# A two-block transformer in float32 on one core: the statistics of its wide norms held with tokens on the partitions

## The chip, the cores and the metric

One core of a Trainium2 chip runs the whole program, one launch. The metric is device time in microseconds (us) of one execution, lower is better.

## What is computed

256 tokens of width 2048 go through two transformer blocks. The first mixes three branches (a gated convolution, chunked attention, attention over 256 memory tokens) and has a gated feed-forward part. The second has adaptive norms (shift and scale from a conditioning vector), four attention mixers of 512 columns each and a mixture of 16 experts. What matters here are the norms over all 2048 features:

```python
def rmsnorm(x, g):
    xf = x.astype(jnp.float32)
    y = xf * lax.rsqrt(jnp.mean(xf * xf, axis=-1, keepdims=True) + EPS)
    return (y * g.astype(jnp.float32)).astype(x.dtype)

    h = h + merged @ w_o[l]
    hn = rmsnorm(h, ffn_norm_g[l])                               # "ffn"
    ...
    h = h + (jax.nn.silu(gt) * val) @ w_down[l]
    return rmsnorm(h, final_norm_g)                              # "final"
    ...
    h = rmsnorm_2(x, norm1_g[l]) * (1.0 + sc1[:, None]) + sh1[:, None]   # "norm1"
    x = x + g1[:, None] * token_mixer(h, ...)
    h = rmsnorm_2(x, norm2_g[l]) * (1.0 + sc2[:, None]) + sh2[:, None]   # "norm2"
    x = x + g2[:, None] * moe_ffn(h, ...)
    return rmsnorm_2(x, final_g)                                 # "final2"
```

`norm1` follows `final` directly, so the kernel takes both roots at one place and applies `final` to the carried stream later.

## The kernel before

Activations lie with features on the 128 partitions and the 256 tokens along the free axis, 16 chunks of 128 features. Each f32 weight tile (128x2048) is split by ScalarE into a rounded part `w_hi` (`split`, L603) and by VectorE into the rest `w_lo` (`lo`, L1942); TensorE multiplies with both. Activations are split in the same way into `a_hi` and `a_lo`. There are four raw and four split buffers, and each engine's program is written out in order by hand: PE's block from L1192, VectorE's from L1929, ScalarE's from L595. Engines meet only through semaphores, and a wait holds up everything behind it on its engine.

A norm's sum of squares is taken over partitions: PE multiplies a 128x128 matrix of ones with the squares (`run_lane` L1370, `run_last` L1375). That gives the sum of every token in a full row of 256, the same on all 128 partitions (`psN`, in the bank `psO`). `root` (L1959 to L1963) forms mean plus EPS on 128x256 elements (VectorE), waits for ScalarE's square root (`std`, L712), and takes the reciprocal into `rstd` (L1962). `by_pairs` (L1981) then multiplies the 16 prescaled chunks two at a time by `rstd` and splits them, while ScalarE writes the upper parts (L701, L707). `root_both` (L1968 to L1974) does the same for `norm1` (a second row in `psM`) and leaves `final`'s root in `var`; its reciprocal is taken at step 11 of the second block's loop (L2536) and is applied from step 18 on. Behind the sums PE issues products of ones that nobody reads (`idle_products`, L1197): 14 at `ffn` and at `norm1`, 20 at `norm2`, none at `final2`, and 9 ahead of tile 3 of the second block.

The second block's loop runs over 58 weight tiles, step n for tile n, on PE (`second_half`, L1722), VectorE (L2521) and ScalarE (L1041). PE takes tiles 0 and 1 together. VectorE's step n first makes `w_lo` of tile n + 3. Before its step 0 it waits until ScalarE has copied out tile 0, and writes an input of the compression there (`cmp_in`, L2448). Its step 0 ends with L2458, its step 1 with a second `cmp_in`. ScalarE's `w_hi` of tile n + 4 waits for PE's end of tile n. At steps 5 and 7 PE turns the result of a gelu that VectorE makes from tile 3 and tile 5 (L1625).

Of the kernel before, what the change touches and what calls it, by code (L numbers as in the profile page):

```python
# [19 lines left out]
ALU = mybir.AluOpType  # L20
# [3 lines left out]
P = 128  # L24
S = 256
# [280 lines left out]

ROOTS = ["mem", "x", "lnvar", "ffn", "norm1", "final", "mixb", "mixd", "mixa", "mixc", "norm2", "final2"]
ROOT_AT = {n: k for k, n in enumerate(ROOTS)}
# [13 lines left out]
ADA_FIRST = 6  # L322
ADA_EACH = 9


# [5 lines left out]
def build(nc, tiles, ada_tiles, x_d, mem_d, params_d, crow_d, rel_rev, onehot_d, maskrow_d, ident_d,  # L331
          cmpmask_d, tab_d, sinks_d, rbias_d, router_d, gd_d, w2_d, pe_d, grp_d, tri_d, out, fbias_d):
    with ExitStack() as ctx:
# [6 lines left out]
        def sem(name):  # L340
# [34 lines left out]
        psF = psT[:, 0, 0:S]  # L375
        psM = psO[:, S:2 * S]

        landed = [sem(f"tile_landed{s}") for s in range(RAW)]
# [16 lines left out]
                 "gain_last_squares", "gain_sums", "rstd_ready", "normed_pairs", "tail_chunk",  # L395
                 "carried", "pre_ready", "rstd_columns", "rstd_columns_copied", "conv_lane", "centred_lane", "first_hi", "first_lo"]
        W = {n: sem(n) for n in names}
# [53 lines left out]
        def col(n):  # L451
            _cols[0] += n
            return small[:, _cols[0] - n:_cols[0]]
# [15 lines left out]
        cs = col(12)  # L469
        rcol = col(2)  # L470
        iota = col(NE)
        warm_root = col(1)
# [123 lines left out]
        def _(act):  # L596
# [301 lines left out]
            for k in range(DC):  # L898
# [8 lines left out]
            std("ffn")  # L907
            act.wait_ge(used, BASE["ffn"])
# [26 lines left out]
            def ffn_groups():  # L935
# [65 lines left out]

            act.wait_ge(W["variance_ready"], NORM_AT["norm1"] + 1)
            nc.scalar.activation(pool[:, VAR2, :], pool[:, VAR2, :], ACT.Sqrt, bias=zero, scale=1.0 / D)\
                .then_inc(W["std_ready"], 1)
            std("final")
            split(Tile(BASE["two"] + 2))
# [81 lines left out]
            for g in range(4):  # L1088
# [3 lines left out]
                for c in range(4 * g, 4 * g + 4):  # L1092
                    if g == 3:
                        if c < 15:
                            act.wait_ge(W["tail_chunk"], 3 + c - 11)
                        else:
# [3 lines left out]
                                         scale=scale2[:, c:c + 1]).then_inc(W["pre_ready"], 1)  # L1100
            std("norm2")
            act.wait_ge(used, BASE["moe"])
# [73 lines left out]
            for g in range(4):  # L1176
# [3 lines left out]
                for c in range(4 * g, 4 * g + 4):  # L1180
                    if g == 3:
                        if c < 15:
                            act.wait_ge(W["tail_chunk"], 6 + c - 11)
                        else:
# [3 lines left out]
                                         scale=pc("final2_g", c)).then_inc(W["pre_ready"], 1)  # L1188
            std("final2")


        @block.tensor  # L1192
        def _(pe):
            def idle_products(n, into=None):

                for _ in range(n):
                    nc.tensor.matmul(psS[:, 1, 0:P] if into is None else into, ones[:, :], ones[:, :],  # L1197
                                     start=True, stop=True)
# [158 lines left out]
            def norm_part(name, g, sq=SQ, into=psN):  # L1357
# [6 lines left out]
                last.then_inc(W["sums_part"], 1)  # L1364

            def run_lane(name, lane, into=psN, start=True):

                wait(pe, W["variance_ready"], NORM_AT[name])
                pe.wait_ge(W["lanes_added"], 3 * RUN.index(name) + 3)
                nc.tensor.matmul(into, ones[:, :], pool[:, lane, :], start=start, stop=False)  # L1370

            def run_last(name, c, sq, into=psN):

                pe.wait_ge(W["last_squares"], 4 * RUN.index(name) + c + 1)
                last = nc.tensor.matmul(into, ones[:, :], pool[:, sq + 4 + c, :], start=False,  # L1375
                                        stop=c == 3 and name != "final")
                if c == 3:
                    last.then_inc(W["sums_part"], 3)
# [160 lines left out]
            run_last("ffn", 3, SQ)  # L1539
            idle_products(14)  # L1540

            def ffn_groups():
# [42 lines left out]
                for c in range(4):  # L1585
                    nc.tensor.matmul(psM, ones[:, :], pool[:, GAIN_SQ + c, :], start=c == 0, stop=False)
                pe.wait_ge(W["gain_lanes"], 2)
                nc.tensor.matmul(psM, ones[:, :], pool[:, GAIN_LANE, :], start=False, stop=False)
                wait(pe, W["variance_ready"], NORM_AT["final"])
                for c in range(4):  # L1590
                    if c == 3:
                        pe.wait_ge(W["lanes_added"], 3 * RUN.index("final") + 3)
                        nc.tensor.matmul(psN, ones[:, :], pool[:, FINAL_LANE, :], start=False, stop=False)
                    run_last("final", c, US)
                    pe.wait_ge(W["gain_last_squares"], c + 1)
                    last = nc.tensor.matmul(psM, ones[:, :], pool[:, GAIN_SQ + 4 + c, :], start=False, stop=c == 3)
                last.then_inc(W["gain_sums"], 1)
                idle_products(14)

# [324 lines left out]
            for n in range(4):  # L1924
                big_down(NE - 1, n)
            run_sums("final2", HF, 56, psF)


        @block.vector  # L1929
        def _(dve):  # L1930
# [24 lines left out]
            def root(name, width, src=psN):  # L1955
# [7 lines left out]
                dve.wait_ge(W["rstd_ready"], ROOT_AT[name] + 1)  # L1963

            def root_both():

                dve.wait_ge(W["gain_sums"], 1)
                nc.vector.tensor_scalar(var[:, :], psN, 1.0 / D, EPS, ALU.mult, ALU.add)\  # L1968
                    .then_inc(W["variance_ready"], 1)
                dve.wait_ge(W["variance_ready"], NORM_AT["final"] + 1)  # L1970
                nc.vector.scalar_tensor_tensor(pool[:, VAR2, :], var[:, :], EPS * D, psM, ALU.mult, ALU.add)\
                    .then_inc(W["variance_ready"], 1)
                dve.wait_ge(W["std_ready"], NORM_AT["final"])
                nc.vector.reciprocal(pool[:, RSTD2, :], pool[:, VAR2, :]).then_inc(W["rstd_ready"], 1)  # L1974
                dve.wait_ge(W["rstd_ready"], ROOT_AT["norm1"] + 1)

# [297 lines left out]
            dve.wait_ge(emptied["D"], OWN[:BASE["ffn"]].count("D"))  # L2274
            root("ffn", D)
            dve.wait_ge(W["pre_ready"], 16)
            by_pairs("ffn", PRE, rstd[:, :])

# [150 lines left out]
            root_both()  # L2429
            by_pairs("norm1", PRE, pool[:, RSTD2, :], bias=mod[:, 0:16])  # L2430
            lo(Tile(BASE["two"] + 2))
# [89 lines left out]
            for n, (kind, what, x) in enumerate(SECOND):  # L2521
# [58 lines left out]
                .then_inc(W["router_lo"], 1)  # L2580
            root("norm2", D)
            dve.wait_ge(W["pre_ready"], 32)
            by_pairs("norm2", PRE, rstd[:, :], bias=mod[:, 48:64])
            dve.wait_ge(W["router_turned"], 1)
# [136 lines left out]
            for n in range(4):  # L2721
                expert_add(NE - 1, n)
            root("final2", D, psF)
            dve.wait_ge(W["pre_ready"], 48)
            for p in range(8):
                y = chunks(PRE + 2 * p, 2)
                nc.vector.tensor_tensor(y, y, rstd[:, :].unsqueeze(1).to_broadcast([P, 2, S]), ALU.mult)\
                    .then_inc(W["final_ready"], 1)
# [259 lines left out]
```

## Time and profile before

| | us |
|---|---|
| median of 3 runs | 2922.99 |
| lowest and highest | 2920.28, 2929.36 |
| the profiled execution, its own time | 2924.94 |
| its span, first to last instruction | 2923.1 |
| PE (TensorE) busy | 2864.7 (98%) |
| DVE (VectorE) busy | 2171.5 (74%) |
| ACT (ScalarE) busy | 1510.5 (52%) |
| one split of a weight tile, mean: ScalarE, VectorE | 1.91, 2.30 |

The profile is of one execution. A page gives busy times, a picture of the span in 40 slices, the chain of work that ended last, and the costliest groups of instructions; the trace behind it can be asked for the instructions of a stretch in order of time. An f32 product appears as two records (two passes). Ends of PE's records are modelled and overlap, so starts are the safer numbers. The granted clock is 1.00 at TensorE's full 2.4 GHz and 0.50 at 1.2 GHz.

### The profile page before, as it was taken

Reading aid. Unit: us, or ns where it says so; the run is one execution under the profiler, and the core shown is the slowest. Engines: PE = TensorE matmul, PEld = TensorE weight load, DVE = VectorE, ACT = ScalarE, POOL = GpSimd, SP = SyncE. Lnnn points to the kernel's source line nnn. Section 1 sums busy time; section 2 is a strip of 40 time slices with the busy share of each in tenths; the row PEclk is TensorE's granted clock in tenths of the full one; section 3 lists DMA queues with packets and bytes.
Section 4 is the critical chain, followed back from the end, with each engine's and each line's share of the span. In section 5 each row is a group of like instructions: output and inputs, shape, how many; then the busy total and the mean of one; then the engine's idle time right before and its main releaser. Section 6 shows DMA issues by size and latency. Waiting matters only on the chain.

```text
span 2923.1 us, 45813 instructions
## 1 busy us (share of the span) xinstructions
PE 2864.7 (98%) x18030; PEld 2582.3 (88%) x18030; DVE 2171.5 (74%) x2675; ACT 1510.5 (52%) x1716; POOL 157.6 (5%) x228
## 2 busy tenths in 40 slices
PE   8999999999999999999999999999999999999998
PEld 8888888888888899999999989998989889889887
DVE  5644459998875899999999984665865876875874
ACT  5444564445554544444444464556554664664763
POOL 3000010000101000000000020111010000000001
PEclk9999999999999999999999999999999999999999
DMA  7445445555463978888788756444325885885982
GB/s 282 174 157 183 169 160 179 184 185 187 172 233 130 366 310 323 323 329 329 315 328 329 293 174 248 172 156 156 133 86 218 332 329 216 336 314 215 356 313 78
DMA packets 115681, 692.27 MB, mean 237 GB/s; under 512 B 14240, under 2 KB 27792, under 8 KB 34768
## 3 DMA queue, kind: packets, MB, share of 16 engines
q1 hardware_dynamic: 109952, 675.33, 61.1%
q10 hardware_dynamic: 4688, 11.01, 1.2%
q0 software_dynamic: 896, 3.93, 0.4%
q8 instruction: 99, 1.62, 0.2%
q14 instruction: 46, 0.38, 0.0%
HBM read 679.74 MB, written 10.49 MB: 236 GB/s over the span
## 4 chain that ended last, share of the span: by engine, by line
PE 88%; DVE 6%; ACT 3%; issue 2%; DMA 1%; SPq 0%; DVEq 0%; ACTq 0%
PE psT L1223 22%; PE psT L1224 11%; PE psT L1210 6%; PE psT L1212 6%; PE psT L1211 6%; PE psT L1332 3%; PE psT L1826 3%; PE psT L1828 3%; PE psT L1827 3%; PE psT L1816 2%; PE psT L1815 2%; PE psT L1817 2%; DVE w_lo L1942 2%; PE psY L1867 1%; PE psY L1866 1%
## 5 line engine op out<-in xcount | busy, mean ns | idle before, releaser
L1942 DVE TENSOR_TENSOR w_lo<-raw,w_hi 128x2048 fp32r<-128x2048 f32 x532 | 1220.0, 2297 | 369.4 <-ACT w_hi L603 364.8
L603 ACT ACTIVATE w_hi<-raw 128x2048 fp32r<-128x2048 f32 x532 | 1015.5, 1910 | 394.9 <-PE psT L1212 133.5
L1223 PE MATMUL psT<-a_both,w_hi 128*128 128x512 f32 x3072 | 1092.6, 400 | 9.6 <-DVE a_both L1992 2.8
L1224 PE MATMUL psT<-a_both,w_lo 128*128 128x256 f32 x3072 | 863.4, 281 | 0.0
L1223 PEld LDWEIGHTS psT<-a_both,w_hi 128*128 128x128 f32 x3072 | 578.7, 188 | 152.8 <-issue 8.7
L1224 PEld LDWEIGHTS psT<-a_both,w_lo 128*128 128x128 f32 x3072 | 581.7, 189 | 0.3
L1210 PE MATMUL psT<-a_both,w_hi 128*128 128x256 f32 x784 | 228.8, 292 | 9.2 <-DVE pool L2103 4.4
L1212 PE MATMUL psT<-a_both,w_lo 128*128 128x256 f32 x784 | 223.8, 285 | 0.0
L1211 PE MATMUL psT<-a_both,w_hi 128*128 128x256 f32 x784 | 223.6, 285 | 0.0
L2289 DVE CUSTOM_DVE_ANT_0 pool<-pool 128x2048 f32<-128x2048 f32 x96 | 219.0, 2281 | 4.9 <-DVE mod L2299 4.9
L1210 PE MATMUL psT<-h_hi,w_hi 128*128 128x256 f32 x752 | 214.7, 286 | 1.8 <-DVE pool L2305 1.1
L1211 PE MATMUL psT<-h_lo,w_hi 128*128 128x256 f32 x752 | 213.2, 284 | 0.0
L1212 PE MATMUL psT<-h_hi,w_lo 128*128 128x256 f32 x752 | 213.1, 283 | 0.0
L1210 PEld LDWEIGHTS psT<-a_both,w_hi 128*128 128x128 f32 x784 | 152.3, 194 | 10.7 <-DVE w_lo L1942 4.6
L1211 PEld LDWEIGHTS psT<-a_both,w_hi 128*128 128x128 f32 x784 | 152.3, 194 | 0.3
L1212 PEld LDWEIGHTS psT<-a_both,w_lo 128*128 128x128 f32 x784 | 152.1, 194 | 0.0
L1826 PE MATMUL psT<-w_hi,xw_hi 128*128 128x512 f32 x384 | 150.7, 393 | 0.0
L1828 PE MATMUL psT<-w_hi,xw_lo 128*128 128x512 f32 x384 | 149.6, 389 | 0.0
L1827 PE MATMUL psT<-w_lo,xw_hi 128*128 128x512 f32 x384 | 149.5, 389 | 0.0
L1210 PEld LDWEIGHTS psT<-h_hi,w_hi 128*128 128x128 f32 x752 | 144.8, 193 | 4.0 <-DVE pool L2305 1.4
L1815 PE MATMUL psT<-a_both,w_hi 128*128 128x256 f32 x512 | 146.0, 285 | 0.0
L1816 PE MATMUL psT<-a_both,w_hi 128*128 128x256 f32 x512 | 145.4, 284 | 0.0
(390 smaller groups left out, 4606.9 us busy)
## 6 DMA issues: line engine op xcount, KB each, us to landing
raw<-tiles_dram SPq DMA_DIRECT2D x532, 1024.0 KB, 5.0
pool<-ada_tiles_dram SPq DMA_DIRECT2D x96, 1024.0 KB, 4.9
bias_rows_dram<-pool ACTq DMA_DIRECT2D x1, 8192.0 KB, 56.5
pool<-bias_rows_dram SPq DMA_DIRECT2D x40, 128.0 KB, 4.5
pool<-bias_rows_dram SPq DMA_DIRECT2D x40, 64.0 KB, 4.6
pool<-mem_dram SPq DMA_DIRECT2D x4, 512.0 KB, 8.0
raw<-tiles_dram SPq DMA_DIRECT2D x8, 256.0 KB, 8.0
pool<-x_dram ACTq DMA_DIRECT2D x1, 2048.0 KB, 11.1
```

Source lines behind the costliest of these rows:

```text
L603: nc.scalar.activation(w_hi[:, t.k % SPL, :], raw[:, t.k % RAW, :], ACT.Copy).then_inc(hi_done, 1)
L1210: nc.tensor.matmul(ps_out, wh, x_hi, start=first, stop=False)
L1211: nc.tensor.matmul(ps_out, wh, x_lo, start=False, stop=False)
L1212: return nc.tensor.matmul(ps_out, wl, x_hi, start=False, stop=last)
L1223: nc.tensor.matmul(dst.rearrange("p (h s) -> p h s", h=2), wh, a_both[:, :, a, :], start=first, stop=False)
L1224: return nc.tensor.matmul(dst[:, 0:S], wl, a_hi[:, a, :], start=False, stop=last)
L1815: nc.tensor.matmul(dst, wh, a_hi[:, k, :], start=k == 0 and n % 2 == 0, stop=False)
L1826: nc.tensor.matmul(dst, xw_hi[:, k, :], wh, start=k == 0, stop=False)
L1827: nc.tensor.matmul(dst, xw_hi[:, k, :], wl, start=False, stop=False)
L1828: last = nc.tensor.matmul(dst, xw_lo[:, k, :], wh, start=False, stop=k == DC - 1)
L1942: nc.vector.tensor_tensor(w_lo[:, t.k % SPL, :], raw[:, t.k % RAW, :], w_hi[:, t.k % SPL, :].bitcast(F32), ALU.subtract).then_inc(lo_done, 1)
L2289: nc.vector.tensor_tensor_reduce(out=buf, in0=buf, in1=flat(CROW, 8), scale=1.0, scalar=0.0, op0=ALU.mult, op1=ALU.add, accum_out=ada_acc[ ...
```

## The change

For `ffn`, `norm1`, `final`, `norm2` and `final2` the squares become the stationary operand and one column of ones the moving one: two products 128x1 per chunk, one for each 128 tokens. The sums then stand in two columns, tokens on the partitions. Mean, root and reciprocal work on 128x2 elements in `small`. PE spreads the two columns back: `stat_rows` uses the column, broadcast to 128x128, as weights and the identity as moving operand, into `psRows` (part of `psP`, a PSUM bank), and VectorE's multiplications read their factor there. The four narrow mixer norms and those ahead of `ffn` stay as they were.

```diff
+            def token_std(name, at=0, scale=1.0):
+                act.wait_ge(W["variance_ready"], NORM_AT[name] + 1)
+                nc.scalar.activation(stat[:, at:at + 2], stat[:, at:at + 2], ACT.Sqrt, bias=zero, scale=scale)\
+                    .then_inc(W["std_ready"], 1)
...
+            def token_sums(into, src, start=False, stop=False):
+                for tt in range(2):
+                    last = nc.tensor.matmul(into[:, tt:tt + 1], src[:, tt * P:tt * P + P], ones[:, 0:1],
+                                            start=start and tt == 0, stop=stop and tt == 1)
+                return last
+
+            def stat_rows(name):
+                pe.wait_ge(W["stat_ready"], STATS.index(name) + 1)
+                for tt in range(2):
+                    last = nc.tensor.matmul(psRows[:, tt * P:tt * P + P],
+                                            stat_r[:, tt:tt + 1].to_broadcast([P, P]), ident[:, :], start=True, stop=True)
+                last.then_inc(W["stat_rows"], 1)
...
             run_last("ffn", 3, SQ)
-            idle_products(14)
+            idle_products(8)
+            stat_rows("ffn")
+            idle_products(6)
...
                 last.then_inc(W["gain_sums"], 1)
-                idle_products(14)
+                idle_products(8)
+                stat_rows("norm1")
+                idle_products(8)
...
                     gelu_turned(n // 7)
+                if n == 2:
+                    stat_rows("final")
                 second_half(n, 0)
...
             run_sums("norm2")
-            idle_products(20)
+            idle_products(8)
+            stat_rows("norm2")
+            idle_products(12)
...
             run_sums("final2", HF, 56, psF)
+            stat_rows("final2")
...
+            def rows_of(name, at):
+                nc.vector.reciprocal(stat_r[:, 0:2], stat[:, at:at + 2]).then_inc(W["stat_ready"], 1)
+                dve.wait_ge(W["stat_rows"], STATS.index(name) + 1)
+
+            def token_root(name, src=psN):
+                m = NORM_AT[name]
+                dve.wait_ge(W["sums_part"], SQ_AT[name] + GROUPS[name])
+                nc.vector.tensor_scalar(stat[:, 0:2], src[:, 0:2], 1.0 / D, EPS, ALU.mult, ALU.add)\
+                    .then_inc(W["variance_ready"], 1)
+                dve.wait_ge(W["std_ready"], m + (1 if m < NORM_AT["lnmean"] else 0))
+                rows_of(name, 0)
...
-            by_pairs("ffn", PRE, rstd[:, :])
+            by_pairs("ffn", PRE, psRows)
...
                 attend(SECOND_UNITS, 20, SC2, Q2, ticks_at(n, 0, N_UNITS + 4))
-                if n == 11:
+                if n == 1:
                     dve.wait_ge(W["std_ready"], NORM_AT["norm1"])
-                    nc.vector.reciprocal(rstd[:, :], var[:, :]).then_inc(W["rstd_ready"], 1)
+                    rows_of("final", 0)
+                    nc.vector.tensor_copy(rstd[:, :], psRows).then_inc(W["rstd_ready"], 1)
                     dve.wait_ge(W["rstd_ready"], ROOT_AT["final"] + 1)
```

Where instructions move, their order tells more than the diff. VectorE, steps 0 and 1 of the second block's loop, before: `w_lo` of tile 3, `h_lo`, `w_lo` of tile 4, the second `cmp_in`.

```order
L1942 TENSOR_TENSOR w_lo<-raw,w_hi 128x2048 [waits tile_hi_done]
L2458 TENSOR_TENSOR h_lo<-pool,h_hi 128x480 [waits cmp_hi]
L1942 TENSOR_TENSOR w_lo<-raw,w_hi 128x2048 [waits tile_hi_done]
L2448 TENSOR_TENSOR pool<-pool 64x8x15 [waits cmp_lo,sums_emptied_act]
L2448 TENSOR_TENSOR pool<-pool 64x8x15 x7
L1942 TENSOR_TENSOR w_lo<-raw,w_hi 128x2048 [waits tile_hi_done] x2
```

The same place in the changed kernel (each line number is the new file's):

```order
L1981 TENSOR_TENSOR w_lo<-raw,w_hi 128x2048 [waits tile_hi_done]
L2510 TENSOR_TENSOR h_lo<-pool,h_hi 128x480 [waits cmp_hi]
L1981 TENSOR_TENSOR w_lo<-raw,w_hi 128x2048 [waits tile_hi_done]
L2006 RECIPROCAL small<-small 128x2 [waits std_ready]
L2589 COPY rstd<-psY 128x256 [waits stat_rows]
L2500 TENSOR_TENSOR pool<-pool 64x8x15 [waits cmp_lo,sums_emptied_act,rstd_ready]
L2500 TENSOR_TENSOR pool<-pool 64x8x15 x7
L1981 TENSOR_TENSOR w_lo<-raw,w_hi 128x2048 [waits tile_hi_done] x2
```

Behind `w_lo` of tile 4 there is now the small reciprocal, and a copy that waits for PE.

PE at the same place in the changed kernel, from the end of tile 1 to the start of tile 2:

```order
L1220 MATMUL psT<-a_both,w_hi 128x256
L1221 MATMUL psT<-a_both,w_lo 128x256
L1386 MATMUL psY<-ident,small 128x128 [waits stat_ready,tile_lo_done]
L1386 MATMUL psY<-ident,small 128x128
L1219 MATMUL psT<-a_both,w_hi 128x256 [waits sums_emptied_act,tile_lo_done]
L1220 MATMUL psT<-a_both,w_hi 128x256
```

The two spreading products stand ahead of tile 2; before, L1212 of tile 1 was followed directly by L1210 of tile 2.

PE behind the sums of `norm2`, before:

```order
L1370 MATMUL psY<-pool,ones 128x256 [waits lanes_added,variance_ready]
L1375 MATMUL psY<-pool,ones 128x256 [waits last_squares] x4
L1197 MATMUL psY<-ones 128x128 x20
L1610 MATMUL psY<-a_both,h_hi 16x256 [waits ident_r_set,act_lo_ready,variance_ready,router_lo]
```

and in the changed kernel, from the last chunk's squares on:

```order
L1378 MATMUL psY<-ones,pool 128x1 [waits last_squares]
L1378 MATMUL psY<-ones,pool 128x1
L1206 MATMUL psY<-ones 128x128 x8
L1386 MATMUL psY<-ident,small 128x128 [waits stat_ready]
L1386 MATMUL psY<-ident,small 128x128
L1206 MATMUL psY<-ones 128x128 x12
L1644 MATMUL psY<-a_both,h_hi 16x256 [waits ident_r_set,act_lo_ready,variance_ready,router_lo]
```

The spreading products stand behind eight idle ones, and twelve follow them ahead of the router's first product.

## Rows read from the trace of the kernel before

**Rows 1.** Page, part 4: shares by engine of the chain that ended last.

```profile
PE 88%; DVE 6%; ACT 3%; issue 2%; DMA 1%; SPq 0%; DVEq 0%; ACTq 0%
```

**Rows 2.** Timeline at `norm2` (start us, us, engine, line, op, tiles, shapes, count, [idle before]).

```profile
2150.78 0.67 PE L1375 MATMUL psY<-pool,ones 128*128 128x256 f32 x2 [0.19 <-ACT pool L679]
...
2151.29 4.63 PE L1197 MATMUL psY<-ones 128*128 128x128 f32 x40
2151.49 0.43 DVE L1959 TENSOR_SCALAR var<-psY 128x256 f32<-128x256 f32 x1 [2.19 <-PE psY L1375]
2151.95 0.42 ACT L712 ACTIVATE var<-var 128x256 f32<-128x256 f32 x1 [0.82 <-DVE var L1959]
...
2152.40 1.75 DVE L1962 RECIPROCAL rstd<-var 128x256 f32<-128x256 f32 x1 [0.48 <-ACT var L712]
2154.19 1.29 DVE L1981 TENSOR_TENSOR pool<-pool,rstd 128x512 f32<-128x512 f32 x2
```

**Rows 3.** Groups by form on VectorE: busy us, mean ns of one | idle before.

```profile
L2231 DVE TENSOR_TENSOR pool<-psT,pool 128x512 f32<-128x512 f32 x24 | 16.5, 689 | 13.2 <-ACT pool L861 13.2
...
L2038 DVE TENSOR_SCALAR small<-small 128x2 f32<-128x2 f32 x68 | 11.5, 169 | 2.4
...
L2054 DVE RECIPROCAL small<-small 128x2 f32<-128x2 f32 x68 | 10.8, 159 | 0.5
L1981 DVE TENSOR_TENSOR pool<-pool,rstd 128x512 f32<-128x512 f32 x16 | 10.8, 683 | 0.1
```

**Rows 4.** Group by form on ScalarE.

```profile
L747 ACT ACTIVATE small<-small 128x1 f32<-128x1 f32 x16 | 4.5, 280 | 0.0
```

**Rows 5.** Timeline, PE: 128x1 products on f32 weights, two tiles of tokens.

```profile
62.42 0.50 PE L1477 MATMUL psY<-ident,rstd 128*128 128x1 f32 x4
```

**Rows 6.** Timeline at `ffn`.

```profile
939.97 3.29 PE L1197 MATMUL psY<-ones 128*128 128x128 f32 x28
940.99 0.42 DVE L1959 TENSOR_SCALAR var<-psY 128x256 f32<-128x256 f32 x1
...
943.67 1.29 DVE L1981 TENSOR_TENSOR pool<-pool,rstd 128x512 f32<-128x512 f32 x2
```

**Rows 7.** Timeline at `final2`, the end of the program.

```profile
2912.07 0.42 DVE L1959 TENSOR_SCALAR var<-psT 128x256 f32<-128x256 f32 x1 [2.52 <-PE psT L1375]
...
2914.76 4.90 DVE L2727 TENSOR_TENSOR pool<-pool,rstd 128x512 f32<-128x512 f32 x8
```

**Rows 8.** Timeline at `norm1`.

```profile
1713.98 3.29 PE L1197 MATMUL psY<-ones 128*128 128x128 f32 x28
1714.43 0.41 DVE L1968 TENSOR_SCALAR var<-psY 128x256 f32<-128x256 f32 x1
...
1717.66 1.29 DVE L1981 TENSOR_TENSOR pool<-pool 128x512 f32<-128x512 f32 x2
...
1719.62 0.35 PE L1210 MATMUL psT<-a_both,w_hi 128*128 128x256 f32 x1 [2.35 <-DVE a_both L2005]
```

**Rows 9.** Timeline on VectorE, start of the second block's loop.

```profile
1733.01 2.60 DVE L2448 TENSOR_TENSOR pool<-pool 64x120 f32<-64x120 f32 x8 [1.32 <-ACT pool L1077]
...
1738.42 2.28 DVE L1942 TENSOR_TENSOR w_lo<-raw,w_hi 128x2048 fp32r<-128x2048 f32 x1
```

**Rows 10.** Timeline on PE, same place.

```profile
1733.05 0.36 PE L1210 MATMUL psT<-a_both,w_hi 128*128 128x256 f32 x1 [0.21 <-ACT pool L1077]
...
1738.87 2.17 PE L1197 MATMUL psY<-ones 128*128 128x128 f32 x18
```

**Rows 11.** Timeline on PE, start of tile 5 of the second block.

```profile
1752.04 0.24 PE L1625 MATMUL psY<-ident,pool 30*128 30x30 f32 x1 [2.32 <-DVE pool L2474]
```

**Rows 12.** Windows: us, busy (x instructions) of PE, PEld, DVE, ACT, POOL, granted clock, DMA, GB/s.

```profile
2178.00:2180.00 2.00, 1.87 (x10) 1.88 (x10) 0.07 (x1) 0.00 (x0) 0.00 (x0) 0.50 0.96 406
...
2186.00:2188.00 2.00, 2.00 (x12) 2.00 (x11) 1.79 (x2) 2.00 (x2) 0.00 (x0) 0.52 1.01 426
...
1720.00:1724.00 4.00, 4.00 (x23) 4.00 (x23) 4.00 (x10) 2.68 (x7) 0.00 (x0) 0.57 0.00 0
```

More of the change, by code:

```diff
@@ L305 @@
     _at += GROUPS[_name]
-ROOTS = ["mem", "x", "lnvar", "ffn", "norm1", "final", "mixb", "mixd", "mixa", "mixc", "norm2", "final2"]
+ROOTS = ["mem", "x", "lnvar", "final", "mixb", "mixd", "mixa", "mixc"]
 ROOT_AT = {n: k for k, n in enumerate(ROOTS)}
@@ L323 @@
 ADA_EACH = 9
+STATS = ["ffn", "norm1", "final", "norm2", "final2"]
 def ada_place(k):
@@ L376, in build @@
         psM = psO[:, S:2 * S]
+        psRows = psP[:, 0:S]
         landed = [sem(f"tile_landed{s}") for s in range(RAW)]
@@ L470, in build @@
         rcol = col(2)
+        stat, stat_r = col(4), col(4)
         iota = col(NE)
@@ L906, in _ @@
                                      scale=pc("ffn_norm_g", k)).then_inc(W["pre_ready"], 1)
-            std("ffn")
+            token_std("ffn")
             act.wait_ge(used, BASE["ffn"])
@@ L1000, in _ @@
             ffn_groups()
[L1002 to L1005, printed above, removed]
+            token_std("norm1", 2, 1.0 / D)
+            token_std("final")
             split(Tile(BASE["two"] + 2))
@@ L1100, in _ @@
                                          scale=scale2[:, c:c + 1]).then_inc(W["pre_ready"], 1)
-            std("norm2")
+            token_std("norm2")
             act.wait_ge(used, BASE["moe"])
@@ L1188, in _ @@
                                          scale=pc("final2_g", c)).then_inc(W["pre_ready"], 1)
-            std("final2")
+            token_std("final2")
         @block.tensor
@@ L1369, in run_lane @@
                 pe.wait_ge(W["lanes_added"], 3 * RUN.index(name) + 3)
+                if name in STATS:
+                    token_sums(into, pool[:, lane, :], start)
+                    return
                 nc.tensor.matmul(into, ones[:, :], pool[:, lane, :], start=start, stop=False)
@@ L1374, in run_last @@
                 pe.wait_ge(W["last_squares"], 4 * RUN.index(name) + c + 1)
-                last = nc.tensor.matmul(into, ones[:, :], pool[:, sq + 4 + c, :], start=False,
-                                        stop=c == 3 and name != "final")
+                stop = c == 3 and name != "final"
+                if name in STATS:
+                    last = token_sums(into, pool[:, sq + 4 + c, :], False, stop)
+                else:
+                    last = nc.tensor.matmul(into, ones[:, :], pool[:, sq + 4 + c, :], start=False, stop=stop)
                 if c == 3:
@@ L1592, in ffn_groups @@
                         pe.wait_ge(W["lanes_added"], 3 * RUN.index("final") + 3)
-                        nc.tensor.matmul(psN, ones[:, :], pool[:, FINAL_LANE, :], start=False, stop=False)
+                        token_sums(psN, pool[:, FINAL_LANE, :])
                     run_last("final", c, US)
                     pe.wait_ge(W["gain_last_squares"], c + 1)
-                    last = nc.tensor.matmul(psM, ones[:, :], pool[:, GAIN_SQ + 4 + c, :], start=False, stop=c == 3)
+                    last = token_sums(psM, pool[:, GAIN_SQ + 4 + c, :], False, c == 3)
                 last.then_inc(W["gain_sums"], 1)
-                idle_products(14)
+                idle_products(8)
+                stat_rows("norm1")
+                idle_products(8)
             ffn_groups()
@@ L1963, in root @@
                 dve.wait_ge(W["rstd_ready"], ROOT_AT[name] + 1)
+            def rows_of(name, at):
[8 more added lines that the diff above has]
+                rows_of(name, 0)
             def root_both():
                 dve.wait_ge(W["gain_sums"], 1)
-                nc.vector.tensor_scalar(var[:, :], psN, 1.0 / D, EPS, ALU.mult, ALU.add)\
+                nc.vector.tensor_scalar(stat[:, 0:2], psN[:, 0:2], 1.0 / D, EPS, ALU.mult, ALU.add)\
                     .then_inc(W["variance_ready"], 1)
                 dve.wait_ge(W["variance_ready"], NORM_AT["final"] + 1)
-                nc.vector.scalar_tensor_tensor(pool[:, VAR2, :], var[:, :], EPS * D, psM, ALU.mult, ALU.add)\
+                nc.vector.scalar_tensor_tensor(stat[:, 2:4], stat[:, 0:2], EPS * D, psM[:, 0:2], ALU.mult, ALU.add)\
                     .then_inc(W["variance_ready"], 1)
                 dve.wait_ge(W["std_ready"], NORM_AT["final"])
-                nc.vector.reciprocal(pool[:, RSTD2, :], pool[:, VAR2, :]).then_inc(W["rstd_ready"], 1)
-                dve.wait_ge(W["rstd_ready"], ROOT_AT["norm1"] + 1)
+                rows_of("norm1", 2)
             def by_pairs(name, src, rows, bias=None):
@@ L2274, in _ @@
             dve.wait_ge(emptied["D"], OWN[:BASE["ffn"]].count("D"))
-            root("ffn", D)
+            token_root("ffn")
             dve.wait_ge(W["pre_ready"], 16)
-            by_pairs("ffn", PRE, rstd[:, :])
+            by_pairs("ffn", PRE, psRows)
             nc.vector.memset(us[:, :, 0:2], 0.0).then_inc(W["pairs_read"], 2)
@@ L2429, in _ @@
             root_both()
-            by_pairs("norm1", PRE, pool[:, RSTD2, :], bias=mod[:, 0:16])
+            by_pairs("norm1", PRE, psRows, bias=mod[:, 0:16])
             lo(Tile(BASE["two"] + 2))
@@ L2580, in _ @@
                 .then_inc(W["router_lo"], 1)
-            root("norm2", D)
+            token_root("norm2")
             dve.wait_ge(W["pre_ready"], 32)
-            by_pairs("norm2", PRE, rstd[:, :], bias=mod[:, 48:64])
+            by_pairs("norm2", PRE, psRows, bias=mod[:, 48:64])
             dve.wait_ge(W["router_turned"], 1)
@@ L2722, in _ @@
                 expert_add(NE - 1, n)
-            root("final2", D, psF)
+            token_root("final2", psF)
             dve.wait_ge(W["pre_ready"], 48)
@@ L2726, in _ @@
                 y = chunks(PRE + 2 * p, 2)
-                nc.vector.tensor_tensor(y, y, rstd[:, :].unsqueeze(1).to_broadcast([P, 2, S]), ALU.mult)\
+                nc.vector.tensor_tensor(y, y, psRows.unsqueeze(1).to_broadcast([P, 2, S]), ALU.mult)\
                     .then_inc(W["final_ready"], 1)
```

6 lines of the change are left out of this document (3 added, 3 removed).

## Prediction

> **What bounds the kernel now.** I read the chain of work that ended last first: 88% of it is PE [rows 1]. A change pays only where PE stands still or where its last work is released late, and it costs wherever it makes PE wait. The norms are such places: PE has nothing to multiply until the first chunks are normalised. So I read the four norms in order of time, then the stretch of the second block into which the change puts a new wait.
>
> At `norm2` [rows 2] the reader is to see a relay. The last squares go through PE at 2150.78, VectorE adds EPS at 2151.49 (0.43 us), ScalarE takes the root at 2151.95 (0.42), VectorE the reciprocal at 2152.40 (1.75), and the first multiplication starts at 2154.19. That is 2.70 us from sum to use, 1.75 of it one reciprocal of 256 elements. Beside it run 40 records of idle products, 4.63 us, 0.116 each. At `ffn` the same relay takes 943.67 - 940.99 = 2.68 us [rows 6], at `norm1`, with one step more, 1717.66 - 1714.43 = 3.23 [rows 8], at `final2` 2914.76 - 2912.07 = 2.69 [rows 7].
>
> **The small steps.** On 128x2 elements VectorE needs 0.17 us for a tensor_scalar and 0.16 for a reciprocal [rows 3]. For the root I take 0.28, from the nearest row, 128x1 on ScalarE [rows 4]. With hand-overs of 0.03 to 0.04 us, as between the rows of `norm2`, this makes 0.17 + 0.04 + 0.28 + 0.03 + 0.16 = 0.68 us. Then the spreading is new: two f32 products, four records. Four records of 128x1 took 0.50 us [rows 5]; with 128 moving columns at 0.116 each and the drain of the last I take 0.6, between 0.5 and, at half the clock, 1.0. The sums themselves: two products of 128x1 per chunk are four records, 0.50 us, instead of two records of 256 columns, 0.67 us [rows 2, 5]. The last sum comes 0.15 us sooner, and PE's time is the same within 0.02 us per chunk, which I leave out.
>
> The multiplications now read their factor in PSUM. A tensor_tensor of this shape with one operand in PSUM takes 689 ns, without one 683 ns [rows 3]; I cost this at nothing (8 x 6 ns at `final2`). The Trainium skill speaks against it: "VectorE: DVE Perf Modes", section on the TRN2 errata, gives a fixed 120 cycles at 0.96 GHz for a PSUM source and 58 for SBUF, by which (an estimate) each multiplication would cost 65 ns more, `final2` 0.5 us, and the total would come out 0.5 us or a little more above mine. Here the rows decide: 6 ns.
>
> **Norm by norm.** The spreading products stand behind eight idle products, 16 records, and PE works in order. So each start is the later of two times.
>
> - `ffn`: the small steps are through at 940.99 + 0.68 = 941.67. The idle products start at 939.97, 0.118 each, and eight are through at 941.85. Plus 0.6 and a hand-over: 942.5 instead of 943.67, a gain of 1.2. What follows is a relay of VectorE and ScalarE that sets when PE gets its next tiles, so I let it through whole.
> - `norm1`: 1714.43 + 0.68 + 0.21 for the second small step = 1715.32. Idle products: 1713.98 + 1.88 = 1715.86. Start 1716.5 instead of 1717.66, a gain of 1.15.
> - `norm2`: the small steps end at 2152.0, but eight idle products only at 2151.29 + 1.86 = 2153.15. Start 2153.8 instead of 2154.19, a gain of 0.4. The twelve idle products behind may hold the router's first product some tenths longer, but its last one waits for VectorE. Bounds 0 and 0.6.
> - `final2`: no idle products. 2912.07 - 0.15 + 0.68 = 2912.6, 0.1 until PE has it, 0.6 to spread: 2913.3 to 2913.4 instead of 2914.76. I take 1.3; at half the clock 0.95. Nothing runs beside it, so it reaches the end whole.
>
> **`final`, the new wait.** Here the change does more than it says. The reciprocal that leaves step 11 (again 1.75 us of VectorE, as in [rows 2]; it lay beside a busy PE) gains nothing. But PE must now have the result of VectorE's step 1 before it may begin tile 2. Before, PE began tile 2 at 1733.05 [rows 10], and VectorE ended `w_lo` of tile 4 only at 1738.42 + 2.28 = 1740.70 [rows 9].
>
> Step by step. After `norm1` PE had stood idle for 2.35 us [rows 8], and then 4 us ran at a mean granted clock of 0.57 [rows 12], a mix of 2.4 and 1.2 GHz that lost 0.43 x 4 = 1.7 us. Now PE restarts at 1719.62 - 1.15 = 1718.5, and idle products last until about 1718.3; I take it that the clock holds. Tiles 0 and 1 end 1.15 + 1.7 = 2.85 us sooner, near 1729.7. VectorE's first `cmp_in` waits for ScalarE's copy of tile 0; VectorE itself is free 1.32 us before 1733.01 [rows 9], less 1.15, at 1730.6. So it starts there, 2.4 sooner. Everything behind it follows, and `w_lo` of tile 4 ends at 1738.3. Reciprocal 0.16, hand-over and four records 0.55: tile 2 starts at 1739.0, **5.95 us later** than before, after PE has stood still for some 8.8 us. Queued behind the wait on PE is all of the second block; VectorE in turn waits for the spreading and copies 128x256 (0.4 us) ahead of the second `cmp_in`, which is no later than before.
>
> After that pause the clock will be low. The nearest row is the 1.7 us above, and I take it; the far one is 2178 to 2188 [rows 12], where the clock stayed at 0.50 for nearly 10 us after a pause, 4.8 us lost. Against this, PE had waited 2.32 us for the gelu at 1752.04 [rows 11]. From the end of tile 3 that work now needs a split by ScalarE and one by VectorE, 1.91 and 2.30 in the table of the profile, and some 1.1 us of small steps, 5.3 (an estimate), and PE spends 5.8 on tile 4, as on tile 2 (1738.87 - 1733.05). The wait should vanish: -2.3. Net at this place 5.95 + 1.7 - 2.3 = **+5.35**.
>
> **Sum.** -1.2 (`ffn`) + 5.35 (`norm1` and `final` together) - 0.4 (`norm2`) - 1.3 (`final2`) = +2.45 us. On the profiled execution's 2924.94 that makes 2927.4, on the median of 2922.99 it makes 2925.4; the profiled execution lies 1.95 above the median. I say **2926**. A measurement of this kernel tells about 0.3%, 8.8 us, from no change, so this is no difference.
>
> **Rivals.**
>
> *The wait costs nothing* (0.10). VectorE or the order leaves PE unhindered at tile 2. For it speaks that VectorE was idle 26% of the span; against it, the two orders at this place and the 7.65 us between 1733.05 and 1740.70. Then the change gives what its norms promise: -1.2 - 2.4 - 0.4 - 1.3 = -5.3, 2917.7.
>
> *The norms gain only at the end* (0.15). PE's spreading is slower than I think (idle products in front, the drain, a lower clock), and VectorE starts where it started. Then the new wait is also longer: tile 2 at 1740.70 + 0.71 = 1741.4, +8.35 + 1.7 - 2.3 = 7.75, less 1.3 makes +6.45, 2929.4.
>
> *Slower beyond doubt* (0.08). One mechanism: PE's pause drops the clock for as long as at 2178 to 2188, 4.8 us, and the gelu waits stay, since VectorE's and ScalarE's steps move with PE. Then 5.95 + 4.8, nothing recovered, and a second gelu wait of 2.3 at tile 7: 13.05, less 1.2 and 0.95: +10.9, 2933.9. It decides from a cost of 11 us at this place. The Trainium skill has the rule behind it ("TensorE: Matmul & The Clock Gate", section "Why this matters for your kernels"): avoid idle gaps between bursts of products, or the engine falls to half its rate. Rows 12 show the two levels; how long the fall lasts is what I can't read ahead.
>
> **How the numbers follow.** My own case has 0.67, with some 2 us either way for the spreading and the clock, and runs of this kernel spread by 4 us around their median. The low end takes in the first rival, the high end the second and part of the third: 2918 to 2933. Faster by over 0.3% is below 2914, beyond every case but scatter: 0.03. Slower by over 0.3% is above 2931.8: the third rival and a tail of the second, 0.09. The rest, 0.88, is no difference.
>
> **What would show it.** Right: between VectorE's sum and its first multiplication 1.5 us at `ffn`, 2.1 at `norm1`, 2.4 at `norm2`, 1.4 at `final2`; ahead of tile 2 a pause of PE of 8 to 9 us that ends with VectorE's reciprocal, then a stretch at 1.2 GHz, and no wait at L1625. No low clock after `norm1`. Wrong: a pause under 3 us there, a gap at `norm2` of 1.4, which would mean that PE overtakes its idle products, or the lost time turning up in the experts' stage, which I have left untouched.

## The result, and the profile after

Against 7 runs of the kernel before (median 2924.38 us), 7 runs of the changed kernel have a median of 2937.99 us (2933.58 to 2946.72): a ratio of 1.0047, 95% interval 1.0029 to 1.0066. That is 13.6 us slower by the medians. The forecast of 2926.0 and its upper end of 2933 both lie below it.

The chain that ended last, part 4 of the changed kernel's page, has less PE than before [rows 1]:

```profile
PE 86%; DVE 6%; ACT 3%; issue 2%; DMA 2%; SPq 0%; DVEq 0%; ACTq 0%
```

The profiled execution took 2933.58 us, span 2931.8, 8.7 more than before. Where those 8.7 us lie is read from the two traces, place by place. Timeline of the changed kernel at `ffn` (start us, us, engine, line, op, tiles, shapes, count, [idle before]):

```profile
937.07 2.84 PE L1206 MATMUL psY<-ones 128*128 128x128 f32 x16
938.22 0.15 DVE L2013 TENSOR_SCALAR small<-psY 128x2 f32<-128x2 f32 x1
938.41 0.30 ACT L718 ACTIVATE small<-small 128x2 f32<-128x2 f32 x1 [1.37 <-DVE small L2013]
938.74 0.17 DVE L2006 RECIPROCAL small<-small 128x2 f32<-128x2 f32 x1 [0.37 <-ACT small L718]
...
939.70 1.06 PE L1386 MATMUL psY<-ident,small 128*128 128x128 f32 x4
...
940.80 1.28 DVE L2033 TENSOR_TENSOR pool<-pool,psY 128x512 f32<-128x512 f32 x2 [1.89 <-PE psY L1386]
```

The small steps are as forecast: through at 938.91, 0.69 us after they began (0.68). But the eight idle products (16 records) last 2.84 us instead of 1.9, and the spreading 1.06. Sum to first multiplication: 2.58 us, against 2.68 before [rows 6] and 1.5 forecast. At `norm1`, same view:

```profile
1705.08 7.90 PE L1378 MATMUL psY<-ones,pool 128*128 128x1 f32 x56
...
1712.84 3.70 PE L1206 MATMUL psY<-ones 128*128 128x128 f32 x16
1713.01 0.16 DVE L2021 TENSOR_SCALAR small<-psY 128x2 f32<-128x2 f32 x1 [1.38 <-PE psY L1378]
...
1713.73 0.17 DVE L2006 RECIPROCAL small<-small 128x2 f32<-128x2 f32 x1 [0.36 <-ACT small L718]
...
1716.37 0.61 PE L1386 MATMUL psY<-ident,small 128*128 128x128 f32 x4
...
1717.02 1.28 DVE L2033 TENSOR_TENSOR pool<-pool,psY 128x512 f32<-128x512 f32 x2 [3.12 <-PE psY L1386]
```

Here 2.47 us pass between the end of the small steps (1713.90) and the spreading, all of it idle products. The windows of the changed kernel (us, busy (x instructions) of PE, granted clock, DMA share, GB/s) say why:

```profile
1706.00:1708.00 2.00, 2.00 (x20) 1.00 0.00 0
1708.00:1710.00 2.00, 2.00 (x18) 0.88 0.00 0
1710.00:1712.00 2.00, 2.00 (x11) 0.50 0.00 0
1712.00:1714.00 2.00, 2.00 (x10) 0.50 0.54 172
```

PE counts as fully busy, and still the granted clock has fallen to 1.2 GHz in the middle of the one-column sums. In the kernel before, it stood at 1.00 over this stretch. Low clocks also stand at the other norms; at `final2`, the last row, PE was busy for only 1.22 of the 2 us:

```profile
938.00:940.00 2.00, 2.00 (x12) 0.53 0.00 0
...
2161.00:2163.00 2.00, 2.00 (x12) 0.50 0.00 0
2922.00:2924.00 2.00, 1.22 (x4) 0.50 0.00 0
```

Ahead of tile 2 of the second block, PE's timeline shows the new wait:

```profile
1738.75 1.19 PE L1386 MATMUL psY<-ident,small 128*128 128x128 f32 x4 [8.04 <-DVE small L2006]
1739.60 0.56 PE L1219 MATMUL psT<-a_both,w_hi 128*128 128x256 f32 x1
...
1747.22 2.17 PE L1206 MATMUL psY<-ones 128*128 128x128 f32 x18
```

The last of these rows, the idle products of tile 3, stands at 1738.87 in [rows 10].

The table cuts all traces at the same instructions; each entry is the difference of two starts. "Relay" is from VectorE's first step on the sums to its first multiplication. The last four columns are versions from the section below.

| us | before | after | e1 late | e2 wide | e3 both | e6 fewer |
|---|---|---|---|---|---|---|
| relay `ffn` | 2.68 | 2.58 | 1.49 | 1.48 | 1.49 | 1.50 |
| `ffn` to the sums of `norm1` | 770.76 | 772.21 | 772.82 | 770.77 | 770.74 | 770.74 |
| relay `norm1` | 3.23 | 4.01 | 4.48 | 2.19 | 2.18 | 1.67 |
| first multiplication to the gelu's product | 34.38 | 40.98 | 34.94 | 40.88 | 35.02 | 35.40 |
| gelu to the sums of `norm2` | 399.45 | 400.99 | 401.04 | 400.95 | 399.90 | 400.68 |
| relay `norm2` | 2.70 | 3.35 | 4.48 | 2.24 | 2.24 | 1.50 |
| experts, to the sums of `final2` | 757.88 | 759.07 | 759.22 | 767.84 | 761.00 | 759.49 |
| relay `final2` | 2.69 | 2.00 | 2.00 | 1.50 | 1.50 | 1.50 |

The changed kernel's rows are 11.4 us longer in sum. Its span is only 8.7 longer because it was 2.8 us ahead before `ffn`, in untouched code: 936.02 against 938.79 at the last `w_lo`. This stretch and the experts' are where executions of one kernel differ: the experts' took 761.00 us in e3 and 758.53 in e8, which are one kernel. In e2's trace PE waits 4.08 us near 2578 for VectorE, whose steps there stand behind an expert's tile that came late by DMA:

```profile
2572.99 1.91 ACT L608 ACTIVATE w_hi<-raw 128x2048 fp32r<-128x2048 f32 x1 [2.44 <-DMA raw<-tiles_dram]
```

So one profile says little by its span, and much by the rows between.

### The profile page after: what moved, and what is told of

It reads as the page before. It is cut to its first block, busy times and chain, and to the rows that moved or that the text cites. A ratio compares the mean times of both kernels' runs of the same rounds, so it can differ in the third digit from the quotient of the medians.

```text
span 2931.8 us, 45974 instructions
## 1 busy us (share of the span) xinstructions
PE 2872.3 (98%) x18112; PEld 2595.7 (89%) x18112; DVE 2163.8 (74%) x2676; ACT 1509.9 (52%) x1716; POOL 157.3 (5%) x228
## 4 chain that ended last, share of the span: by engine, by line
PE 86%; DVE 6%; ACT 3%; issue 2%; DMA 2%; SPq 0%; DVEq 0%; ACTq 0%
PE psT L1232 21%; PE psT L1233 11%; PE psT L1219 6%; PE psT L1220 6%; PE psT L1221 6%; PE psT L1341 3%; PE psT L1866 3%; PE psT L1864 3%; PE psT L1865 3%; DVE w_lo L1981 2%; PE psT L1853 2%; PE psT L1855 2%; PE psT L1854 2%; ACT w_hi L608 2%; DMA raw<-tiles_dram 2%
## 5 line engine op out<-in xcount | busy, mean ns | idle before, releaser
L1233 PE MATMUL psT<-a_both,w_lo 128*128 128x256 f32 x3072 | 862.6, 281 | 0.0
L1219 PE MATMUL psT<-a_both,w_hi 128*128 128x256 f32 x784 | 229.4, 293 | 6.2 <-DVE w_lo L2167 3.3
L1220 PE MATMUL psT<-a_both,w_hi 128*128 128x256 f32 x784 | 224.4, 286 | 0.0
L1221 PE MATMUL psT<-a_both,w_lo 128*128 128x256 f32 x784 | 224.3, 286 | 0.0
L1853 PE MATMUL psT<-a_both,w_hi 128*128 128x256 f32 x512 | 145.6, 284 | 0.5 <-DVE w_lo L1981 0.5
L1855 PE MATMUL psT<-a_both,w_lo 128*128 128x256 f32 x512 | 144.9, 283 | 0.0
```

Of the source, the lines that this page charges most:

```text
L1219: nc.tensor.matmul(ps_out, wh, x_hi, start=first, stop=False)
L1220: nc.tensor.matmul(ps_out, wh, x_lo, start=False, stop=False)
L1221: return nc.tensor.matmul(ps_out, wl, x_hi, start=False, stop=last)
L1233: return nc.tensor.matmul(dst[:, 0:S], wl, a_hi[:, a, :], start=False, stop=last)
L1853: nc.tensor.matmul(dst, wh, a_hi[:, k, :], start=k == 0 and n % 2 == 0, stop=False)
```

## The experiments

Two theories. **The clock:** sums with one moving column let PE's clock fall, and idle products, spreading and sums then run at half rate. **The wait:** PE's pause of 8 us ahead of tile 2 is the bulk of the cost. Rival to both: the cost comes from elsewhere, or the other theory bears it alone.

**e1, the wait moved.** At step 1 VectorE takes only the small reciprocal; PE spreads `final` ahead of step 4; VectorE copies the rows at its step 4.

```
-                if n == 2:
+                if n == 4:
                     stat_rows("final")
...
                 if n == 1:
                     dve.wait_ge(W["std_ready"], NORM_AT["norm1"])
-                    rows_of("final", 0)
+                    nc.vector.reciprocal(stat_r[:, 0:2], stat[:, 0:2]).then_inc(W["stat_ready"], 1)
+                if n == 4:
+                    dve.wait_ge(W["stat_rows"], STATS.index("final") + 1)
                     nc.vector.tensor_copy(rstd[:, :], psRows).then_inc(W["rstd_ready"], 1)
```

> The changed kernel with one thing moved: PE spreads `final` ahead of step 4 of the second block instead of ahead of step 2, and VectorE takes the small reciprocal at its step 1 without waiting for PE and copies the rows at its step 4. Theory (the wait for VectorE's first step ahead of tile 2 is the bulk of the cost): PE's pause of 8.0 us at tile 2 and the low clock behind it are gone, tile 3's idle products at 1747.2 come 8 us sooner or more, and the total falls by 8 to 10 us, to about 2924 to 2926 where the changed kernel takes 2934. Rival (the cost comes from elsewhere, the pause being absorbed by the gelu wait at L1625): 0 to 3 us less.

**e2, the sums wide.** 128 equal columns instead of one; VectorE reads one of each 128.

```
-                    last = nc.tensor.matmul(into[:, tt:tt + 1], src[:, tt * P:tt * P + P], ones[:, 0:1],
+                    last = nc.tensor.matmul(into[:, tt * P:tt * P + P], src[:, tt * P:tt * P + P], ones[:, :],
                                             start=start and tt == 0, stop=stop and tt == 1)
...
+            def pair_of(row):
+                return row.rearrange("p (t s) -> p t s", t=2)[:, :, 0]
...
-                nc.vector.tensor_scalar(stat[:, 0:2], src[:, 0:2], 1.0 / D, EPS, ALU.mult, ALU.add)\
+                nc.vector.tensor_scalar(stat[:, 0:2], pair_of(src), 1.0 / D, EPS, ALU.mult, ALU.add)\
```

> The changed kernel with the sums made as products of 128x128 instead of 128x1 (128 equal columns, of which VectorE reads one of each 128); everything else as changed, the wait ahead of tile 2 too. Theory (products with one moving column let TensorE's granted clock fall, though the engine counts as busy): clock 1.00 through the sums and idle products of `ffn`, `norm1` and `norm2`; eight idle products in 1.9 us instead of 2.6 to 3.5, spreading in 0.25 to 0.6 us instead of 1.06; sum to first multiplication near 1.5 at `ffn`, 2.1 at `norm1` and 2.2 to 2.4 at `norm2`, and the total 3 to 5 us below the changed kernel. Rival (the clock falls for another reason, or the relay is bound elsewhere): the relays stay at 2.6, 4.0 and 3.35 us and the total within 1 us of the changed kernel.

**e3, both edits.**

> Both edits together: sums with 128 moving columns, `final` spread ahead of step 4. If pause and clock are the two whole causes, the gains forecast for the norms remain: 4 to 6 us below the kernel before. If either theory is wrong, it is no faster than the kernel before, and the one of the two single edits that missed its number shows which.

**e4, the wait alone.** The kernel before; VectorE makes a small reciprocal of ones after the lower half of step 1, and PE waits for it ahead of tile 2. The output is the same; the reciprocal is used by nobody.

```
+                if n == 2:
+                    pe.wait_ge(W["stat_ready"], 1)
+                    idle_products(2)
                 second_half(n, 0)
...
+                if n == 1:
+                    nc.vector.reciprocal(stat_r[:, 0:2], ones[:, 0:2]).then_inc(W["stat_ready"], 1)
```

> The kernel before with the wait alone: PE waits ahead of tile 2 for a small reciprocal that VectorE makes after the lower half of step 1, and then runs two idle products in the place of the spreading; the norms are as before. Theory: the pause costs by itself 5.4 to 9 us (a pause of 8 to 9 us, less what the gelu wait at L1625 gives back). Rival (the cost of the change sits in the norms' slower relays): 0 to 3 us.

Measured on one chip, with 35 runs of the kernel before (median 2924.27); the changed kernel's 2937.99 stands beside 2924.38:

| | median | ratio to before, 95% |
|---|---|---|
| e1 | 2933.01 | 1.0030 [1.0016, 1.0044] |
| e2 | 2930.06 | 1.0023 [1.0011, 1.0036] |
| e3 | 2922.48 | 0.9993 [0.9979, 1.0007] |
| e4 | 2933.72 | 1.0026 [1.0011, 1.0041] |

*The wait.* e4 carries a pause of the same length on otherwise old code. Its PE timeline:

```profile
1736.95 1.20 PE L1198 MATMUL psY<-ones 128*128 128x128 f32 x4 [8.06 <-DVE small L2539]
...
1755.61 0.24 PE L1626 MATMUL psY<-ident,pool 30*128 30x30 f32 x1
...
1760.38 0.41 PE L1633 MATMUL psY<-pool 128*128 128x30 f32 x2 [1.54 <-DVE pool L2483]
```

From `norm1`'s first multiplication to the gelu's product it takes 40.42 us, 6.04 more than the kernel before, where the changed kernel takes 6.60 more. Another 1.58 us follow: from this product to the same one of tile 7 it takes 10.94 us in e4 and in the changed kernel, 9.36 in the kernel before, and PE's new wait of 1.54 us at L1633 lies in between. By the medians e4 costs 9.4, by the ratio in the table 7.6, with an interval of 3 to 12; its experts' stage was 7.6 us longer in the one trace, with a wait of PE at the same place as in e2 (3.23 us). So the wait is shown, at 7.6 us by the rows of the trace.

e1 takes the pause away and gains 6.04 us at this place, 5.0 by the medians. That misses both texts, 8 to 10 and 0 to 3. Part of the reason is in its PE timeline: the gelu wait, which had been absorbed, is back and longer than before [rows 11]. The copy that the edit moved (0.41 us) now stands on VectorE ahead of the gelu's last steps; what it adds to the wait no run separates.

```profile
1738.02 0.66 PE L1386 MATMUL psY<-ident,small 128*128 128x128 f32 x4
...
1748.31 0.27 PE L1659 MATMUL psY<-ident,pool 30*128 30x30 f32 x1 [3.88 <-DVE pool L2526]
```

*The clock.* e2's windows, where the changed kernel had 0.88 and 0.50:

```profile
1708.00:1710.00 2.00, 2.00 (x21) 1.00 0.44 94
1710.00:1712.00 2.00, 1.80 (x17) 1.00 1.01 430
```

and its timeline there:

```profile
1707.62 1.95 PE L1206 MATMUL psY<-ones 128*128 128x128 f32 x16
1707.87 0.15 DVE L2024 TENSOR_SCALAR small<-psY 128x2 f32<-128x2 f32 x1
...
1709.41 0.61 PE L1386 MATMUL psY<-ident,small 128*128 128x128 f32 x4
...
1710.06 1.28 DVE L2036 TENSOR_TENSOR pool<-pool,psY 128x512 f32<-128x512 f32 x2 [1.32 <-PE psY L1386]
```

The idle products last 1.95 us again instead of 3.70, and the relay 2.19 instead of 4.01. All four relays meet their numbers. e2 lies 7.9 below the changed kernel by the medians (6.1 by the table's rows without the experts'), more than the 3 to 5 of the text. At `final2` too its clock is 1.00, with PE busy for 0.71 of the 2 us from 2922. In e1, with one-column sums, the clock was low at `norm1` and `norm2`, whose relays took 4.48 us each; yet at `ffn`, the same code as in the changed kernel, it happened to stay at 1.00 and the relay took 1.49 instead of 2.58. The relay goes with the clock. Nor is this the luck of single profiles, since the mean granted clock of every execution is on record: 0.987 to 0.989 in the 7 of the changed kernel and 0.987 to 0.990 in the 12 of e1, against 0.990 to 0.995 in the 12 of e2, 0.992 to 0.994 in the 12 of e3 and 0.991 to 0.994 in the 35 of the kernel before.

e3 has neither cost: level with the kernel before, where 4 to 6 us less had been expected. In its trace the four relays are 3.9 us shorter in sum than in the kernel before, 1.1 us is given back in the two rows around the gelu, and the experts' stage happened to be 3.1 us longer.

**e5, thin idle products in the kernel before.** Nothing waits for their result, and no sum is touched.

```
-                    nc.tensor.matmul(psS[:, 1, 0:P] if into is None else into, ones[:, :], ones[:, :],
-                                     start=True, stop=True)
+                    dst = psS[:, 1, 0:P] if into is None else into
+                    nc.tensor.matmul(dst[:, 0:1] if n in (14, 20) else dst, ones[:, :],
+                                     ones[:, 0:1] if n in (14, 20) else ones[:, :], start=True, stop=True)
```

> The kernel before, with the idle products behind the sums of `ffn`, `norm1` and `norm2` made 128x1 in the place of 128x128, all else as before; nothing waits for them. Theory (a stretch of products with one moving column lets the granted clock fall, although PE counts as busy all through it): 0.50 in the windows behind `norm1`'s and `norm2`'s idle products, where the kernel before had 1.00 up to the restart, and the first products behind them at half rate; VectorE's relays of 2.7 and 3.2 us unchanged, since they do not wait for PE. Total 0 to 4 us above the kernel before. Rival (the clock falls at the norms because of waits between the sums, not because of their one column): the clock at the norms as in the kernel before, 1.00 until PE stands idle.

Median 2926.45, ratio 1.0008 [0.9995, 1.0020]. Its PE timeline and windows at `norm1` and `norm2`:

```profile
1709.70 3.59 PE L1198 MATMUL psY<-ones 128*128 128x1 f32 x28
...
2147.45 6.92 PE L1198 MATMUL psY<-ones 128*128 128x1 f32 x40
```

```profile
1710.00:1712.00 2.00, 2.00 (x20) 1.00 0.52 74
1712.00:1714.00 2.00, 1.29 (x8) 0.57 0.92 389
2149.00:2151.00 2.00, 2.00 (x12) 0.55 0.00 0
2151.00:2153.00 2.00, 2.00 (x11) 0.50 0.00 0
```

The clock falls within the one-column products, where the kernel before stood at 1.00: at `norm2` with PE busy for 2.00 of 2.00 us, at `norm1` by 1712.5, 0.8 us before they end (0.50 from there to 1713, PE busy all of it). Over the 10 executions of e5 the mean clock was 0.988 to 0.991, beside 0.991 to 0.993 for the kernel before. So it isn't the waits between sums. The relays are the old ones (2.69, 3.23, 2.69 us), since nothing in them waits for PE: a lower clock costs where something stands behind it. The Trainium skill ("TensorE: Matmul & The Clock Gate", section "Why this matters for your kernels") names idle gaps between bursts of products as what drops the rate in mid-kernel. By that rule these stretches should have kept the clock; the rows go against it here.

**e6, fewer idle products ahead of the spreading.** e3, with the split of the idle products moved.

```
-            idle_products(8)
+            idle_products(4)
             stat_rows("norm2")
-            idle_products(12)
+            idle_products(16)
```

and so at `ffn` (4 and 10) and `norm1` (5 and 11).

> The version with both edits (sums of 128 columns, `final` spread ahead of step 4), and fewer idle products ahead of the spreading: four at `ffn` and `norm2`, five at `norm1`, the others moved behind it. Theory (at `norm1` and `norm2` the spreading waits for its idle products, 0.9 us after VectorE's reciprocal at `norm2`): sum to first multiplication 1.4 to 1.5 us at `norm2` instead of 2.24, 1.7 to 1.9 at `norm1` instead of 2.18, `ffn` unchanged at 1.5, clock 1.00 still; 1 to 1.3 us less than with eight, so 3 to 5 below the kernel before. Rival (the short pauses of PE ahead of the spreading drop the clock): 0.50 somewhere there and the relay no shorter.

Median 2919.67 beside 2925.56, ratio 0.9981 [0.9969, 0.9993]. At `norm2`, e6's timeline:

```profile
2146.54 1.06 PE L1206 MATMUL psY<-ones 128*128 128x128 f32 x8
2146.74 0.16 DVE L2016 TENSOR_SCALAR small<-psY 128x2 f32<-128x2 f32 x1 [2.14 <-PE psY L1378]
...
2147.27 0.17 DVE L2009 RECIPROCAL small<-small 128x2 f32<-128x2 f32 x1 [0.37 <-ACT small L718]
...
2147.49 0.71 PE L1386 MATMUL psY<-ident,small 128*128 128x128 f32 x4
...
2148.24 1.29 DVE L2036 TENSOR_TENSOR pool<-pool,psY 128x512 f32<-128x512 f32 x2 [0.80 <-PE psY L1386]
```

PE spreads 0.05 us after the reciprocal, and the relay is 1.50 us. The median, though, gave more than the rows do, so it was measured once more, beside e3.

> The version with wide sums, `final` spread ahead of step 4 and fewer idle products ahead of the spreading, measured once more beside the version with eight. One trace of it showed 2.9 us less than the kernel before outside the experts' stage, its median 5.9 less. If the trace is the right size, this run gives 2 to 4 us less; if the median, 5 to 7. Relays again near 1.5, 1.7, 1.5 and 1.5 us.

> The version with wide sums and `final` spread ahead of step 4, and eight idle products, measured once more: 1 to 3 us less than the kernel before; relays again near 1.5, 2.2, 2.2 and 1.5 us, clock 1.00 at the norms. If the fewer idle products are worth their 1.2 us, this lies that much above the other kernel of this call, which two medians can hardly tell.

Both have a median of 2925.36 beside 2925.11: ratios 0.9996 [0.9984, 1.0008] and 0.9999 [0.9985, 1.0013]. Both fall short of what was expected. The relays repeat to 0.02 us (1.49, 1.67, 1.50, 1.50 with fewer idle products). Over 24 runs of each, every run divided by the median of the kernel before beside it, the median ratio is 0.9988 with fewer idle products and 0.9997 with eight. Outside the experts' stage the four traces lie 2.8 (e3), 2.9 (e6), 4.9 (e7) and 2.2 us (e8) below the one of the kernel before; e3 and e7 owe 1.6 of it to a stretch of low clock that they happen not to have (see the second point below). So the rows say 1 to 2 us with eight and some 3 with fewer. That either version beats the kernel before is not shown, since only one interval of the four leaves out 1. The first median was part scatter.

## Why the prediction was wrong

The forecast was +2.45 us; the rows of the two traces give +11.4. By the steps of the sum:

- **The new wait at tile 2: right.** Counted from `norm1`'s first multiplication, tile 2 starts 7.19 us later (1739.60 - 1717.02 = 22.58 against 1733.05 - 1717.66 = 15.39); forecast 5.95 + 1.15 = 7.10. The low clock behind it costs 1.80 (tile 2 to tile 3's idle products 7.62 against 5.82); forecast 1.7. The gelu wait gives back 2.39 (10.78 from there to the gelu's product, against 13.17); forecast 2.3. Together 6.60 against 6.50. e4 shows the same with the norms untouched. "I take it that the clock holds" was said of the restart after `norm1`, and it held there (1.00 from 1718 to 1724).
- **"The wait should vanish": half right.** It did at L1659, but PE then waits 1.54 us at L1666, at 1762.77, in every trace with the pause (after, e2, e4) and in none without it. The forecast did not ask what would be late next. The row from the gelu to `norm2` is 1.54 longer, all of it here: from the second gelu product on, the changed kernel takes 390.05 us and the kernel before 390.09. In that later part six traces have a stretch of low clock behind one pause of PE and four (e2, e3, e4, e7) have not, and these take 388.48 to 388.54 us instead of 390.05 to 390.39. That is why e4's row is only 0.03 longer. e1's 1.59 more is mostly a low clock behind its gelu wait (0.55 from 1750 to 1752): 1.29 of it stands ahead of the second gelu product. The stretch in the windows of the kernel before, and behind it the same place in e4:

```profile
2032.00:2034.00 2.00, 2.00 (x11) 0.50 0.00 0
```

```profile
2036.00:2038.00 2.00, 2.00 (x16) 1.00 0.47 154
```

  Why it comes in some executions only is open.
- **"PE's time is the same within 0.02 us per chunk, which I leave out": the step that failed.** The four records of 128x1 were priced by their duration alone [rows 5], and the idle products and the spreading behind them at the full clock (0.118 us a record, 0.6 us for four). What the thin products do to the clock of what stands behind them was not asked, though the forecast itself queued the spreading behind 16 records of idle products on the same engine. Instead of -1.2, -1.15, -0.4 and -1.3 the relays changed by -0.10, +0.78, +0.65 and -0.69, and the sums ahead of `norm1` took 1.45 more: 6.1 us in all. e2, which differs in the width of the sums alone, gives 1.48, 2.19, 2.24 and 1.50 us where 1.5, 2.1, 2.4 and 1.4 were forecast. So small steps, spreading and queueing were sized rightly, for a clock that did not hold.
- **The rest**, some 1.3 us, is the experts' stage and the tail. By the medians the change costs 13.6; the two us above the rows lie within the interval, 8.5 to 19.3.
- **A factor read in PSUM costs nothing: right.** The multiplications at `ffn` take 682 ns each against 683 [rows 3], by the changed kernel's groups for the stretch from 930 to 945:

```profile
L2033 DVE TENSOR_TENSOR pool<-pool,psY 128x512 f32<-128x512 f32 x4 | 2.6, 682 | 1.9 <-PE psY L1386 1.9
```

  At `final2` the eight take 4.87 us against 4.90 [rows 7], and from the first of them to the end it is 8.34 us before and 8.39 after. The 0.5 us that the page of the Trainium skill would have added ("VectorE: DVE Perf Modes", section on the TRN2 errata) is not there.

Of the rivals, the second came nearest to the mechanism: a spreading held up by idle products and "a lower clock". But it let this only use up the gain of the relays, where two of them grew, and its longer wait at tile 2 (+8.35) did not come (7.19). The third had nearly the size, 2933.9, by another mechanism: its long low clock behind the pause did not come (1.00 again by 1744). Its 4.8 us for 2178 to 2188 should be 5.0 by the clocks of that stretch (0.50 x 8 + 0.48 x 2) [rows 12]. That a PE busy with the new sums could lose the clock was no case at all, and so the range ended too low.

## What to carry to other kernels

Price a tiny product on TensorE by what it does to the clock of its neighbours, too: here, making the sums 128 times narrower saved nothing and halved the rate of what stood right behind them, and filling the columns again brought it back and cost nothing (`ffn` to the sums of `norm1`: 770.77 us in e2, 770.76 before). Before work is put behind filler on an in-order engine, ask whether something waits for it. And a wait for another engine's result belongs where that result has long been due: moved two steps, `final`'s spreading cost PE no pause at its new place, though its copy on VectorE then stood ahead of the gelu.

## What was not expected of the hardware

- The granted clock falls to 0.50 while PE is busy 2.00 of 2.00 us, while it runs products with one moving column or what stands right behind them (after: 1710 to 1714; e5: 2151 to 2153); with 128 columns in the same place it stays at 1.00 (e2: 1706 to 1712).
- The same code meets it in one execution and not in another: `ffn` took 2.58 us in the changed kernel and 1.49 in e1.
- An f32 product is two records in the profile (40 for 20 idle products [rows 2]); how many passes of the array each stands for no row shows. Four f32 records of 128x128 take 0.61 to 0.71 us at the full clock and 1.06 to 1.22 at the lower one; the relay's small steps of VectorE and ScalarE, 0.15 to 0.30 us each, do not change with it.
